# Modulation products moved from GpSimd to VectorE, and their sums over the partitions made by 32x32 turns and column sums

## The reference, cut to what matters

```
for layer in range(2):
    mod = silu(cond) @ w_mod[layer] + b_mod[layer]        # (1024) @ (1024 x 6144), for both groups
    sh1, sc1, g1, sh2, sc2, g2 = split(mod, 6)
    h = rms_norm(x) * norm_mix[layer] * (1 + sc1) + sh1
    x = x + g1 * mixer(h)                                 # layer 0: hybrid_mixer, layer 1: attention_mixer
    h = rms_norm(x) * norm_ffn[layer] * (1 + sc2) + sh2
    x = x + g2 * conv_ffn(h)
```

## Time and profile before

| | |
|---|---|
| median of 3 runs | 2256.79 us (2255.45 to 2257.45) |
| the profiled execution | 2256.2 us, its span 2254.4 us |
| PE busy | 2025.5 us (90%) |
| DVE busy | 1245.9 us (55%) |
| ACT busy | 801.8 us (36%) |
| POOL busy | 612.0 us (27%) |
| mean granted PE clock | 0.942 of full speed |

### The profile page before, as it was taken

One profiled execution on the slowest core, in us unless ns is written; L12 is line 12 of the kernel. 1 busy time (PEld: TensorE's weight loads), 2 busy tenths in 40 slices (PEclk: granted clock), 3 DMA queues, 4 the chain that ended last, 5 costly groups with the idle time before them and its releaser, 6 DMA issues.

```text
span 2254.4 us, 33757 instructions
## 1 busy us (share of the span) xinstructions
PE 2025.5 (90%) x13441; PEld 1941.2 (86%) x13441; DVE 1245.9 (55%) x1772; ACT 801.8 (36%) x1282; POOL 612.0 (27%) x471
## 2 busy tenths in 40 slices
PE   4898879999897588999999998978889899999998
PEld 3798779999896488999999998966559799999998
DVE  4653773455665757863874746555553654354452
ACT  4543543212221125421432433345542453242341
POOL 0001540000000295989899510353330000000000
PEclk9998999999887698989989998989999799999999
DMA  6221002343230132333333221210001122222221
GB/s 236 89 74 39 20 11 74 112 134 131 96 129 1 56 112 84 121 103 112 121 113 132 89 79 47 71 47 1 1 1 65 47 74 66 74 71 75 78 66 65
DMA packets 54901, 175.78 MB, mean 78 GB/s; under 512 B 7312, under 2 KB 9104, under 8 KB 54416
## 3 DMA queue, kind: packets, MB, share of 16 engines
q1 hardware_dynamic: 52992, 172.06, 22.8%
q10 hardware_dynamic: 1808, 2.36, 0.3%
HBM read 169.92 MB, written 4.47 MB: 77 GB/s over the span
## 4 chain that ended last, share of the span: by engine, by line
PE 57%; DVE 7%; ACT 2%; issue 2%; POOL 2%; DVEq 0%; DMA 0%; ACTq 0%; POOLq 0%
PE ps L348 48%; PE ps L1634 2%; PE ps L1649 2%; PE ps L510 1%; DVE w_lo L341 1%; PE ps L1312 1%; PE ps L1289 1%; DVE PT L1726 1%; DVE yret L1391 1%; PE ps L1295 1%; DVE yret L1359 1%; DVE nmax L1714 1%; ACT w_hi L333 0%; POOL rt L1450 0%; PE ps L1626 0%
## 5 line engine op out<-in xcount | busy, mean ns | idle before, releaser
L341 DVE TENSOR_TENSOR w_lo<-raw,w_hi 128x1024 fp32r<-128x1024 f32 (+1 forms) x237 | 344.6, 1455 | 696.8 <-ACT w_hi L333 696.4
L348 PE MATMUL ps<-h_hi,w_hi 128*128 128x322 f32 x2768 | 655.0, 318 | 35.5 <-DVE h_lo L618 16.1
L348 PE MATMUL ps<-h_lo,w_hi 128*128 128x322 f32 x2768 | 646.6, 315 | 0.0
L348 PE MATMUL ps<-h_hi,w_lo 128*128 128x322 f32 x2768 | 645.7, 315 | 0.0
L333 ACT ACTIVATE w_hi<-raw 128x1024 fp32r<-128x1024 f32 (+1 forms) x237 | 247.0, 1044 | 831.6 <-PE ps L348 816.6
L348 PEld LDWEIGHTS ps<-h_hi,w_hi 128*128 128x128 f32 x2768 | 477.3, 194 | 41.9 <-issue 27.4
L348 PEld LDWEIGHTS ps<-h_lo,w_hi 128*128 128x128 f32 x2768 | 480.2, 194 | 0.0
L348 PEld LDWEIGHTS ps<-h_hi,w_lo 128*128 128x128 f32 x2768 | 476.5, 193 | 0.0
L498 POOL TENSOR_TENSOR maccB<-maccB,mtmp 128x1024 f32<-128x1024 f32 x84 | 225.5, 2684 | 7.0
L491 POOL TENSOR_SCALAR mtmp<-mrawB,csil 128x512 f32<-128x512 f32 x168 | 186.6, 1122 | 46.2 <-DMA mrawB<-in_w_modB 46.2
L348 PE MATMUL ps<-hid_hi,w_hi 128*128 128x322 f32 x704 | 165.2, 316 | 4.3 <-DVE hid_lo L751 4.3
(11 more groups left out here) (256 smaller groups left out, 2355.6 us busy)
## 6 DMA issues: line engine op xcount, KB each, us to landing
raw<-in_ffn_up SPq DMA_DIRECT2D x88, 512.0 KB, 3.3
raw<-in_hyb_in SPq DMA_DIRECT2D x49, 512.0 KB, 3.8
mrawB<-in_w_modB SPq DMA_DIRECT2D x48, 512.0 KB, 4.4
mrawA<-in_w_modB SPq DMA_DIRECT2D x64, 256.0 KB, 2.9
raw<-in_ffn_down SPq DMA_DIRECT2D x32, 448.0 KB, 3.3
raw<-in_w_modA SPq DMA_DIRECT2D x16, 512.0 KB, 4.8
raw<-in_hyb_out SPq DMA_DIRECT2D x16, 512.0 KB, 4.3
raw<-in_ffn_down SPq DMA_DIRECT2D x16, 512.0 KB, 3.5
```

What stands on the lines that cost most here:

```text
L341: dve.tensor_tensor(w_lo[:, i % 2, 0:n], raw[:, b % RAW, 0:n], w_hi[:, i % 2, 0:n].bitcast(F32), SUB).then_inc(S("w_lo"), 1)
L348: last = pe.matmul(pj(f)[:, hh, :], w[:, i % 2, k * 128:(k + 1) * 128], v[:, k, hh * HALF:(hh + 1) * HALF], start=(k == 0 and n == 0), sto ...
```

## The change

All 80 units are done by DVE; POOL has none. Units 32 to 79 come at the end of the DVE bodies listed in `LATE`: every unit of `wo_ret`, every second unit of the up stages of layer 0, every unit of `dn00` and `dn01`, and the first two of `dn02`. For this the DVE loops of layer 0's up stages are written out. The sum over the partitions is made in three steps. DVE turns the 32x32 blocks of each accumulator half (two `transpose`, 128x512) and adds each run of 32 columns (one `tensor_reduce`, 128x1024 to 128x32), which leaves a partial sum for each of the four blocks of partitions in `part`. PE adds the four, with an identity of 32 columns as weights, for many groups at once: groups 0 to 5 before `wo_ssm`, 6 and 7 before the retention, 8 to 19 after `dn02`. modD moves behind the reciprocal of norm10. The modulation loads of SP stand at other places of its list, one for each entry of `LATE`.

```diff
 def macc(q):
-    return maccB[:, (q - QA) % 5, :, :]
+    return maccB[:, q % 2, :, :]
+def sp_mod(sp, m):
+    if m >= 4 * QA + 2:
+        sp.wait_ge(S("mod_mac"), 4 * (m - 1))
+    sp.dma_start(mrawB[:, m % 2, :], ...).then_inc(S(f"ld_mod{m % 2}"), 16)
 def dve_mod_unit(dve, i):
     q, r = i // 4, i % 4
-    if r == 0 and q >= 2:
-        dve.wait_ge(S("mod_cols"), MA // 4 + q - 1)
     ...
+    if r == 3:
+        flip = flipA if q < QA else flipB
+        if q:
+            dve.wait_ge(S("mod_part"), q)
         for g in range(2):
+            dve.wait_ge(S("mod_mac"), 4 * i + 3 + g)
+            dve.transpose(flip[:, 512 * g:512 * g + 512], macc(q)[:, g, :]).then_inc(S("mod_flip"), 1)
+        dve.wait_ge(S("mod_flip"), 2 * q + 2)
+        dve.tensor_reduce(part[:, q, :, :], flip[:, :].rearrange("p (g b c) -> p g b c", g=2, c=32), AX.X, ADD
+                          ).then_inc(S("mod_part"), 1)
-def pool_mod_unit(pool, m): ...
-def pe_mod_sum(pe, q): ...
+def pe_mod_sum(pe, q0, q1):
+    pe.wait_ge(S("mod_part"), q1)
+    n = 8 * (q1 - q0)
+    for t in range(4):
+        last = pe.matmul(B7[32 * t:32 * t + 32, COLS0:COLS0 + n].rearrange("p (q g b) -> p q g b", g=2, b=4),
+                         cst[:, C_ID32:C_ID32 + 32], part[:, q0:q1, :, t:16:4], start=True, stop=True)
+    last.then_inc(S("mod_cols"), 1)
+LATE = [("wo_ret", r) for r in range(8)]
+for n, k in enumerate((8, 8, 2)):
+    LATE += [(f"up0{n}", r) for r in range(1, 2 * PARTS[n], 2)] + [(f"dn0{n}", r) for r in range(k)]
 # dve_out_stage, after dve_residual of unit r; dve_up of layer 0, at the end of the body:
+        dve_late(dve, s, r)
 # pe_ret_in: five pe_mod_sum(pe, q) taken out; then
-pe_mod_sum(pe, 5)
+pe_mod_sum(pe, 0, 6)
 # pe_ret, p == 0
-pe_mod_sum(pe, 6)
-pe_mod_sum(pe, 7)
+pe.wait_ge(S("mod"), 4)
+pe_mod_sum(pe, 6, 8)
 # layer 0's FFN on PE: pe_mod_sum of groups 8 to 19 taken out; then
+pe_mod_sum(pe, 8, 20)
 pe_norm(pe, "norm10")
 # DVE: modB now waits for the sum of groups 0 to 5, modC for that of 6 and 7; modD:
-                if n == 2:
-                    dve_mod(dve, "modD", 24)
 dve_rstd(dve, "norm10")
+dve_mod(dve, "modD", MA // 4 + 3)
 # POOL: the loop over pool_mod_unit and its waits taken out
```

More of the change, by code:

```diff
@@ L39 @@
 C_EPS = C_RPOS + 4
-C_ALL = C_EPS + 1
+C_ID32 = C_EPS + 1
+C_ALL = C_ID32 + 32
 def constants():
@@ L64, in constants @@
     c[:, C_EPS] = EPS
+    c[:, C_ID32:C_ID32 + 32] = (np.arange(128)[:, None] % 32) == np.arange(32)[None]
     return c
@@ L171, in build @@
         hf2 = sb("hf2", [128, 2, TOK])
-        u_sb, t_sb = sb("u_sb", [128, 2, TOK]), sb("t_sb", [128, 2, TOK])
+        u_sb = sb("u_sb", [128, 2, TOK])
+        t_at = nc.sbuf_base
+        t_sb = sb("t_sb", [128, 2, TOK])
         sq, tn = u_sb, t_sb
@@ L241, in build @@
         W = Region(mark + KT * TOK * 4, 28672)
-        mrawB, maccB = W("mrawB", [128, 2, UNIT]), W("maccB", [128, 5, 2, 512])
+        mrawB, maccB = W("mrawB", [128, 2, UNIT]), W("maccB", [128, 2, 2, 512])
+        flipB = W("flipB", [128, UNIT])
+        flipA = nc.alloc_sbuf_tensor_at("flipA", [128, UNIT], F32, offset=t_at)
+        part = Region(A0 + A_BYTES - 2560, 2560)("part", [128, 20, 2, 16])
         yret = Region(A0, mark - A0)("yret", [128, NCH, 1024])
@@ L459, in sp_half @@
                              ).then_inc(S(f"ld_half{k}"), 16)
+        def sp_mod(sp, m):
+            if m >= 4 * QA + 2:
+                sp.wait_ge(S("mod_mac"), 4 * (m - 1))
+            sp.dma_start(mrawB[:, m % 2, :], a["w_modB"][m:m + 1].rearrange("a p n -> (a p) n")).then_inc(S(f"ld_mod{m % 2}"), 16)
         def dve_mod_unit(dve, i):
             q, r = i // 4, i % 4
-            if r == 0 and q >= 2:
-                dve.wait_ge(S("mod_cols"), MA // 4 + q - 1)
             for k in range(2):
-                dve.wait_ge(S(f"ld_half{k}"), 16 * (i + 1))
+                if i < 4 * QA:
+                    w = mrawA[:, k, :]
+                    dve.wait_ge(S(f"ld_half{k}"), 16 * (i + 1))
+                else:
+                    w = mrawB[:, i % 2, k * 512:(k + 1) * 512]
+                    dve.wait_ge(S(f"ld_mod{i % 2}"), 16 * ((i - 4 * QA) // 2 + 1))
                 for g in range(2):
@@ L471, in dve_mod_unit @@
                     if r == 0 and k == 0:
-                        ins = dve.tensor_scalar(acc, mrawA[:, k, :], c, None, MUL)
+                        ins = dve.tensor_scalar(acc, w, c, None, MUL)
                     else:
                         dve.wait_ge(S("mod_mac"), n - 1)
-                        ins = dve.scalar_tensor_tensor(acc, mrawA[:, k, :], c, acc, MUL, ADD)
+                        ins = dve.scalar_tensor_tensor(acc, w, c, acc, MUL, ADD)
                     ins.then_inc(S("mod_mac"), 1)
[L478 to L489, removed]
-                for g in range(2):
[L491 to L510, removed]
-            last.then_inc(S("mod_cols"), 1)
@@ L524, in dve_mod @@
             dve.wait_ge(S("mod_cols"), cols)
-            src = B7[:, COLS0 + 2 * t0:COLS0 + 2 * t1].rearrange("p (m g) -> p m g", g=2)
-            dve.tensor_tensor(ALL_MODS[:, t0:t1, :], src,
-                              ALL_BIAS[:, t0:t1].unsqueeze(2).to_broadcast([128, t1 - t0, 2]), ADD).then_inc(S("mod"), 1)
+            if n:
+                src = B7[:, COLS0:COLS0 + 2 * (t1 - t0)].rearrange("p (q g b) -> p q b g", g=2, b=4)
+                dve.tensor_tensor(ALL_MODS[:, t0:t1, :].rearrange("p (q b) g -> p q b g", b=4), src,
+                                  ALL_BIAS[:, t0:t1].rearrange("p (q b) -> p q b", b=4).unsqueeze(3).to_broadcast([128, (t1 - t0) // 4, 4, 2]),
+                                  ADD).then_inc(S("mod"), 1)
+            else:
+                src = B7[:, COLS0 + 2 * t0:COLS0 + 2 * t1].rearrange("p (m g) -> p m g", g=2)
+                dve.tensor_tensor(ALL_MODS[:, t0:t1, :], src,
+                                  ALL_BIAS[:, t0:t1].unsqueeze(2).to_broadcast([128, t1 - t0, 2]), ADD).then_inc(S("mod"), 1)
             dve.wait_ge(S("mod"), n + 1)
@@ L698, in act_out_stage, with dve_late @@
                     act_square(act, norm, r, x[:, r, :], (tp_read(s, r), f // 2 + 1))
+        LATE = [("wo_ret", r) for r in range(8)]
+        for n, k in enumerate((8, 8, 2)):
+            LATE += [(f"up0{n}", r) for r in range(1, 2 * PARTS[n], 2)] + [(f"dn0{n}", r) for r in range(k)]
+        assert len(LATE) == 80 - 4 * QA
+        def dve_late(dve, s, r):
+            if (s.name, r) in LATE:
+                dve_mod_unit(dve, 4 * QA + LATE.index((s.name, r)))
         def dve_out_stage(dve, s, gate, norm=None, units=None):
@@ L752, in body @@
                                       tile(hid_hi, r // 2 + 2 * j).bitcast(F32), SUB).then_inc(S("hid_ready"), 1)
+                if l == 0:
+                    dve_late(dve, s, r)
+            if l == 0:
+                for r in range(s.M):
+                    body(r, 0)
+                return
             for_units(dve, s, body)
@@ L1795, in _ @@
                             i += 1
-                        late = s.u0 + r - stages["wo_ret"].u0 - 4
-                        if late == 0:
+                        late = s.u0 + r - 4
+                        if late == stages["wo_ret"].u0:
                             sp.wait_ge(S("ret_y"), RH)
                             sp.wait_ge(S("ret_kv"), 4)
-                        if late >= 0 and late % 5 != 4 and m < 80:
-                            sp_mod(sp, m)
-                            m += 1
+                        for t, rt in LATE:
+                            if stages[t].u0 + rt == late:
+                                sp_mod(sp, m)
+                                m += 1
                     continue
@@ L1893, in _ @@
             dve.wait_ge(S("pe_unit"), stages["g"].u0 + 8)
+            dve.wait_ge(S("mod_part"), 6)
             dve_apply(dve, "normS", xsy, lambda k, g: ssmgain[:, k:k + 1], None)
-            dve_mod(dve, "modB", MA // 4 + 6)
+            dve_mod(dve, "modB", MA // 4 + 1)
             dve_out_stage(dve, stages["wo_ssm"], gate(0, 2), None, 24)
             dve_ret_setup(dve)
-            dve_mod(dve, "modC", MA // 4 + 8)
+            dve_mod(dve, "modC", MA // 4 + 2)
             dve_ret(dve)
@@ L1923, in _ @@
             pool_ssd(pool)
[L1924 to L1929, removed]
             pool_tables(pool)
@@ L1952, in _ @@
                 pe_stage(pe, s, H, hready("norm01") if n == 0 else None)
-                for q in ((8, 9, 10, 11), (14, 15, 16), (18, 19))[n]:
-                    pe_mod_sum(pe, q)
                 pe_stage(pe, stages[f"dn0{n}"], HID, ("hid_ready", s.p0))
-                for q in ((12, 13), (17,), ())[n]:
-                    pe_mod_sum(pe, q)
+            pe_mod_sum(pe, 8, 20)
             pe_norm(pe, "norm10")
```

18 lines of the change are left out of this document (1 added, 17 removed).

## The result

The changed kernel takes 2199.04 us (median of 4 runs, 2196.71 to 2200.05), before 2256.12 in the same comparison: ratio 0.9752, 95% interval 0.9738 to 0.9766, or 57 us less. The profiled execution took 2199.0 us with a span of 2197.2 (before 2254.4).

A forecast was written before the change was run, and what follows sets the result against it. PE, busy for 90% of the span, was taken as the bound, so its time and waits count. The terms -43.2 - 8.5 - 5.2 - 0.6 + 2 + 2.2 + 1.6 + 3.2 = -48.5 us gave 2208 us, range 2200 to 2223.

The forecast's parts named there:

- rival D: Whole kernel: larger gain, with DVE's norms and hand-overs earlier and a turn at 0.4 us; 2202 us, chance 0.12.
- no stalls: Up stages: the larger-gain rival's claim that late splits cost PE nothing, -2 us against the forecast.
- groups 0 to 4 in qk, v, g: PE runs there without a gap; taking out five groups of small products at 1.7 us each gives -8.5 us.
- Layer 1's FFN as the control: Layer 0's FFN, 528.5 us, becomes layer 1's 485.3 without PE's sums and POOL's work, if DVE keeps up: -43.2 us.
- The 2 us for late splits: Up stages of layer 0: four groups on odd units, 0.5 us of stall each, +2 us; bounds 0 and 10.
- No gain: Writing out DVE's loops: splits take 1.23 us written out and 1.225 in loops, so no gain and no loss.
- The price of a turn: DVE's turn of 512 columns: 0.65 us, bounds 0.4 and 1.4; a whole group 2.75 us, bounds 2.2 and 4.3.
- rival B: A group costs 4.3 us and the up stages stall: 12.7 us more than forecast, 2221 us, chance 0.14.
- Part (3): Layer 0's FFN: 10.3 of the 43.2 us are clock, lost through the one-column products and regained without them.
- Rival A: Layer 0's FFN: the clock does not come back, being due to position in the kernel; price 10.3 us, 2218.5, chance 0.13.
- Rival C: DVE becomes the bound through a group of 7.7 us, a turn of 3.1; kernel not faster, 2257 and over, chance 0.04.
- The hand-overs: Added DVE work on the path at the ends of g, wo_ssm and wo_ret: +2.2, +1.6 and +3.2 us.

The follow-up runs named there:

- e8: Changed kernel with the old one-column sums on PE, no turns or column sums on DVE, last group summed after up02: 2231.06 us.
- e7: Changed kernel with products of units 32 to 79 back on GpSimd, sums still by turns and column sums on DVE: 2236.04 us.
- e2: Changed kernel plus GpSimd ballast on scratch tiles, same kinds and shapes of instructions as its old late units, results unread: 2340.18 us.
- e4: Changed kernel with turns and column sum made twice in groups 5, 7 and 9 alone, those at the hand-overs: 2204.00 us.
- e5: Changed kernel without modulation work at the last unit of wo_ret, three entries in dn02 instead of two: 2194.56 us.
- e6: Changed kernel with modulation work moved off all three hand-overs, PE adding only groups 0 and 1 before wo_ssm: 2187.24 us.
- e1: Changed kernel with the old one-column sums on PE, no turns or column sums on DVE, last group summed after dn02: 2242.07 us.
- e3: Changed kernel with turns and column sum made twice in the 17 groups other than 5, 7 and 9: 2213.76 us.

## Why the prediction was right, and where it was off

The largest terms came as said and by the causes named, so the forecast was right in its working. The median of 2199.0 lies closer to rival D (2202) than to the forecast (2208), and just under the range. Of D only "no stalls" came true: a group cost 2.55 us and not 2.2. The rest is mostly placement, which no term held: -3.8 in untouched stretches, -2.5 in the retention's loops and +1.3 in `wo_ret`. Without these 5.0 us the time would be 2204, by this count at the edge of the forecast's own 2204 to 2213, so 5 of the 57 us are luck.

The terms of the sum, in us, against the two profiles (said -48.5, measured -57.2 of span):

| term | said | measured |
|---|---|---|
| layer 0's FFN | -43.2 + 2 | -44.3 |
| groups 0 to 4 in qk, v, g | -8.5 | -9.0 |
| gap in front of wo_ssm | +2.2 | +2.2 |
| wo_ssm to the retention's first matmul | +1.6 | +1.2 |
| the retention's loops | 0 | -2.5 |
| its normalisation | -5.2 | -5.1 |
| wo_ret | -0.6 | +1.3 |
| gap in front of up00 | +3.2 | +2.8 |
| all else | 0 | -3.8 |

- Layer 1's FFN as the control: right, and it carried the forecast. The 2 us for late splits were the mis-sized term and measured nothing (no wait for `w_lo`): a group came to 2.55 us instead of 2.75, and the written-out body is faster than the loop's (convolution and `hid_lo` follow their releasers after 0.15 and 0.91 us instead of 0.28 and 1.05). "No gain" for writing out the loops was a small error too.
- The price of a turn: said 0.65 (0.4 to 1.4), measured 0.686; column sum 1.2 against 1.22. The estimate from the bf16 figure of the Trainium skill ("VectorE: DVE Perf Modes", section "The three transpose paths"), 1.24 a turn, was too high by 0.55, and rival B with it.
- Part (3), the clock: the size was right and the cause was right in the main. I put the 10.3 us down to the one-column products; PE's busy time in the six stages fell by 11.0 (489.0 to 478.0). e8 keeps these products with GpSimd silent and pays 8.1 us in the stages behind them. Between before and e8 the stages shrink by 13.9 us, of which 9.3 are waits; of the other 4.6, 3.5 lie in `up00`, which lies ahead of the products and swings by 3 us between kernels (last section). What the prediction left out is that clock is lost without them too, most likely behind PE's longer stalls: e7 has no such products there and pays 6 us. How the 11.0 split between the two in the kernel before is not shown. Rival A did not happen.
- Rival C was priced by the wrong thing. (Its "six times the slowest row" is also off: 6 ns a column is 4.8 times the 1.28 of the copy in the earlier trace rows.) A dear group is not what could have made DVE the bound; GpSimd beside it does, with +141 us in e2. Moving the products while GpSimd is kept busy is the slowest kernel here.
- The hand-overs: the gaps of e4, e5 and e6 show the groups on the path for their full price.
- Of the 8.7 us by which the span fell further than said, 3.1 are in the FFN. 3.8 lie outside what the change touches; the time to the first unit matmul differs there between the ten profiles by 3.8 us (65.5 to 69.2) and the gap in front of z by 3.4 (116.9 to 120.2). The 2.5 in the retention's loops (72.2 to 69.7 us, clock 0.78 to 0.79) are of the same kind: with the same instructions in that stretch the loops took 69.7 us in e2, e5 and e7, 70.5 in e6 and 71.5 to 71.8 in e1, e3, e4 and e8. `wo_ret` lost 1.3 us where 0.6 of gain was said; it took 58.3 to 59.5 us in the other kernels without GpSimd beside it, and its untouched twin `wo` 57.3 to 58.9. What decides between the values stays open.

## What to carry to other kernels

Look in the trace for a stretch that runs the same code without the work in question: the difference in length says what removing that work can give (43.2 us here, 44.3 measured) better than a sum of rows. Count contention on both sides: GpSimd helping VectorE with 434 us of elementwise work slowed it so much that doing the work on VectorE itself was faster (24 us in e8), but only once GpSimd was left idle (e2). Do not judge a cause by the total alone: e8 met the total of the wrong theory, and only the clock stage by stage showed the loss. And put added work into the bodies with slack, not into the last one in front of a norm or a hand-over: 17 groups were nearly free here, the other three and two units of products cost 12 us.

## What the runs showed of the hardware

- A 32x32 turn of 128x512 f32 on DVE takes 0.686 us. That is 1.34 ns a column, near the 1.28 of a copy of 640 columns out of PSUM (0.816 us), and GpSimd beside it does not lengthen it (0.681).
- With GpSimd busy at products of 512 and additions of 1024 columns, the products and the split on DVE, with two SBUF inputs, took 1.8 to 1.9 times as long on average (0.745 to 1.311 us, 1.223 to 2.294), and a `tensor_scalar` with one 1.7 times (0.480 to 0.826).
- Behind a sum of one-column products the clock was low. In the first 10 us after two or three groups of them (3.4 to 8.0 us of PE) it was 0.76 to 0.86 in e8, and 1.00 at the same places without them.
- The clock's return after a hand-over differs between kernels whose code there is alike. Layer 1's `up10` is the same in all ten profiles, behind the same gap of 13.83 us, and takes 120.5 to 123.1 us. In the third 10 us of `up00` the clock was 0.73 in the changed kernel and PE got through 51 matmuls; in e4 it was 1.00, with 69. Such a swing is 2 to 3 us a stage, which no step of the prediction could place, and with 2.9 us in `up00` and 0.9 in `wo_ssm` it is most of why an addition of 7.8 us showed as 5.0.
